# S5 loop: TensorE takes the two parts of each input matrix apart and adds them in PSUM, instead of VectorE adding them first

## What is computed

```python
a_r, a_i = mag * cos(lam_im * dt), mag * sin(lam_im * dt)
bb = coef * b                                  # complex, per group of 16 channels
bur, bui = einsum('gnh,btgh->btgn', bb, u)     # 64 groups, 64 complex states
x = associative_scan(a, bu) in chunks          # state over time
y = einsum('ghn,btgn->btgh', c_re, xr) - einsum('ghn,btgn->btgh', c_im, xi)
y = gelu(y + d * u)
```

## Time and profile before

| | us |
|---|---|
| median of 2 runs | 1878.67 |
| the two runs | 1875.09, 1882.25 |
| the profiled execution | 1876.33 |
| its span, first to last instruction | 1874.2 |
| TensorE busy | 1827.6 |
| VectorE busy | 850.5 |
| ScalarE busy | 778.3 |
| GpSimd busy | 883.0 |

### The profile page before, as it was taken

How to read it: one execution, slowest core, us unless ns; L and a number is a source line. 1 busy time by engine, 2 the same in 40 slices (tenths; PEclk the granted TensorE clock), 3 DMA queues, 4 the chain that set the end, 5 groups by cost and what they waited for, 6 DMA issues and landing times.

```text
span 1874.2 us, 24848 instructions
## 1 busy us (share of the span) xinstructions
PE 1827.6 (98%) x8784; PEld 1480.2 (79%) x8784; DVE 850.5 (45%) x1251; ACT 778.3 (42%) x1262; POOL 883.0 (47%) x1167
## 2 busy tenths in 40 slices
PE   5999999999999999999999999999999999999998
PEld 3688888888888777888888888788888878777876
DVE  8974232121126798432121126761355551477652
ACT  8854343232334567443232334423332342344663
POOL 1015455555545431555555545675454445573123
PEclk8899999999999999999999999999999999899999
DMA  5354243332333221334332323353322323241111
GB/s 193 101 178 149 90 144 103 91 101 90 101 92 99 88 74 39 91 101 146 90 101 90 101 92 93 92 168 90 90 79 79 90 70 106 65 124 57 35 57 56
DMA packets 56036, 182.50 MB, mean 97 GB/s; under 512 B 7200, under 2 KB 7584, under 8 KB 55312
## 3 DMA queue, kind: packets, MB, share of 16 engines
q1 hardware_dynamic: 52416, 174.44, 30.7%
q10 hardware_dynamic: 3536, 6.92, 1.1%
HBM read 165.93 MB, written 6.29 MB: 92 GB/s over the span
## 4 chain that ended last, share of the span: by engine, by line
PE 36%; POOL 29%; issue 28%; DVE 3%; ACT 2%; DMA 1%; POOLq 0%; SPq 0%; ACTq 0%; DVEq 0%
POOL wlo L550 29%; PE ps L1083 8%; PE ps L1085 7%; PE ps L1084 7%; PE ps L1477 2%; PE ps L1476 2%; PE ps L1475 2%; PE ps L1594 1%; PE ps L1584 1%; PE ps L1585 1%; PE ps L1132 1%; PE ps L1331 1%; PE ps L1148 1%; PE ps L1299 1%; PE ps L1522 0%
## 5 line engine op out<-in xcount | busy, mean ns | idle before, releaser
L550 POOL TENSOR_TENSOR wlo<-raw,whi 128x256 fp32r<-128x256 f32 x1136 | 860.0, 793 | 940.5 <-ACT whi L605 830.8
L605 ACT ACTIVATE whi<-raw 128x1024 fp32r<-128x1024 f32 x284 | 297.9, 1052 | 392.9 <-PE ps L1085 347.7
L1083 PE MATMUL ps<-Ch,whi 128*128 128x512 f32 x768 | 305.3, 398 | 0.6 <-POOL wlo L550 0.6
L1085 PE MATMUL ps<-Ch,wlo 128*128 128x512 f32 x768 | 299.3, 390 | 0.0
L1084 PE MATMUL ps<-Cl,whi 128*128 128x512 f32 x768 | 299.1, 389 | 0.0
L1083 PE MATMUL ps<-Ah,whi 128*128 128x512 f32 x632 | 251.8, 398 | 1.8 <-DVE Al L1824 1.6
L1083 PE MATMUL ps<-Bh,whi 128*128 128x512 f32 x640 | 250.4, 391 | 0.0
L1085 PE MATMUL ps<-Bh,wlo 128*128 128x512 f32 x640 | 249.0, 389 | 0.0
L1084 PE MATMUL ps<-Bl,whi 128*128 128x512 f32 x640 | 249.0, 389 | 0.0
L1085 PE MATMUL ps<-Ah,wlo 128*128 128x512 f32 x632 | 246.3, 390 | 0.0
L1084 PE MATMUL ps<-Al,whi 128*128 128x512 f32 x632 | 246.0, 389 | 0.0
(11 more groups left out here) (381 smaller groups left out, 2309.1 us busy)
## 6 DMA issues: line engine op xcount, KB each, us to landing
raw<-in_w SPq DMA_DIRECT2D x284, 512.0 KB, 3.6
ple<-ple_park SPq DMA_DIRECT2D x16, 256.0 KB, 3.9
ple_park<-E ACTq DMA_DIRECT2D x11, 256.0 KB, 2.2
u<-in_xch SPq DMA_DIRECT2D x1, 2048.0 KB, 8.5
swap<-vsb SPq DMA_DIRECT2D x16, 128.0 KB, 2.3
swap<-zz SPq DMA_DIRECT2D x16, 128.0 KB, 2.7
h<-in_xfm SPq DMA_DIRECT2D x2, 1024.0 KB, 6.7
out<-v SPq DMA_DIRECT2D x8, 256.0 KB, 2.0
```

Of the source, the lines that this page charges most:

```text
L550: last = nc.gpsimd.tensor_tensor(wlo[:, r, cc], raw[:, r, cc], whi[:, r, cc].bitcast(F32), ALU.subtract)
L605: nc.scalar.activation(whi[:, slot, :], raw[:, slot, :], ACT.Copy).then_inc(hi_ready, 1)
L1083: nc.tensor.matmul(out, whi[:, slot, w], xh, start=first, stop=False)
L1085: return nc.tensor.matmul(out, wlo[:, slot, w], xh, start=False, stop=last)
```

## The change

`inputs(sl)` calls `matrices` with the operation `None`: the sum (L345) and the wait before it are gone. The two products stay unsummed, the first in `E[:, sl%2]`, the second in `G2` for even slices and in `bt` for odd ones. In `transpose_inputs` each transpose becomes two plain fp32 matmuls with the identity moving, one for each part, accumulated in PSUM. In `kernel_products` each matmul becomes two, one for each part, accumulated in PSUM. Before, the second half of slice 6's kernel products ran in slice 7; now all 8 groups of each slice run in their own slice. `outputs(0)`, which writes its second part to `G2`, now waits until the kernel products of slice 6 are done (`e_used` at 7).

```diff
+        def input_parts(sl):
+
+            return E[:, sl % 2, :, :], (G2[:, :, :], bt[:, :].rearrange("p (g n) -> p g n", g=SG))[sl % 2]
...
                     for g in range(4):
-                        last = nc.tensor.transpose(ps[:, 2 + half, g * P:(g + 1) * P], E[:, sl % 2, 4 * half + g, :], C("ident"))
+                        for k, part in enumerate(input_parts(sl)):
+                            last = nc.tensor.matmul(ps[:, 2 + half, g * P:(g + 1) * P], part[:, 4 * half + g, :], C("ident"), start=(k == 0), stop=(k == 1))
                     last.then_inc(et_ps, 1)
 
             def kernel_products(sl, first, end):
                 for g in range(first, end):
                     gg = sl * SG + g
-                    last = nc.tensor.matmul(ps[:, gg // 32, gg % 32 * GH:(gg % 32 + 1) * GH], E[:, sl % 2, g, :], bC[:, 0, gg * GH:(gg + 1) * GH],
-                                            start=True, stop=True)
+                    for k, part in enumerate(input_parts(sl)):
+                        last = nc.tensor.matmul(ps[:, gg // 32, gg % 32 * GH:(gg % 32 + 1) * GH], part[:, g, :], bC[:, 0, gg * GH:(gg + 1) * GH],
+                                                start=(k == 0), stop=(k == 1))
...
                 pe.wait_ge(c_ready, 1)
-                if sl == NSL - 1:
-                    kernel_products(sl - 1, SG // 2, SG)
-                kernel_products(sl, 0, SG // 2 if sl == NSL - 2 else SG)
+                kernel_products(sl, 0, SG)
...
-                matrices(V, ch, E[:, sl % 2, :, :].rearrange("p g n -> p (g n)"), bt[:, :], pEr, sEi, 0, b1, b2, gs, ALU.add).then_inc(e_ready, 1)
+                one, two = (part.rearrange("p g n -> p (g n)") for part in input_parts(sl))
+                matrices(V, ch, one, two, pEr, sEi, 0, b1, b2, gs, None).then_inc(e_ready, 1)
...
                 if sl == 0:
                     dve.wait_ge(ple_ps, KT)
+                    dve.wait_ge(e_used, NSL - 1)
```

## The result

The changed kernel takes 1911.38 us (median of 1910.42 and 1912.34) against 1878.67 us before: 1.0192 times, 95% interval 1.0176 to 1.0208. It is slower by 1.9%. The forecast was 1898 us with a range of 1889 to 1911; the direction was right, and the time lies 13 us above the forecast and just over the range. The interval takes in 1.02, so it is left open whether the loss passes two per cent.

What follows compares the result with a forecast made beforehand. TensorE was taken to set the pace everywhere in the changed loop. The profiled 1876.3 us plus 15 at full clock plus 7 for clock falls gave 1898 us, with a range of 1889 to 1911.

Steps and rivals of the forecast that it cites:

- What bounds the loop: In the changed loop TensorE sets the pace everywhere: 14.0 us for a three-tile slice, against under 11 for VectorE.
- The gain: VectorE's eight removed sums in the loop make 9.8 us, gained only where TensorE waits for VectorE.
- The price of a pass: TensorE's loop passes at full clock: 0.111 us for transposing products, 0.106 for kernel products; 3.55 and 3.4 us a slice.
- The rival by the factor of four: Transposes in the loop: a plain fp32 matmul costs 0.44 us, not 0.22; total 1926 us, chance within 4%.
- The sum at full clock: TensorE's loop passes add to 94.3 us from 29.3 us; kernel products end at 123.6 us, 16.5 later than before.
- Start, order, tail: Around the loop: first slice gains nothing, reordering and new wait cost nothing, way to the product at 120.31 shrinks 1.6 us.
- The clock: Two falls behind the loop's long 16-column stretches, each some 7 us at half clock, 3.5 us lost: +7 us.
- +17: Upper bound of the loop's clock loss in us: five falls, or three of the long ones.
- The prediction's own sign of being wrong: In the loop: L1110 passes 0.2 us apart at full clock, half clock in most slices, or TensorE still waiting for VectorE.
- The case of a fall behind nearly every stretch: Five or more clock falls behind the loop's kernel products: 1908 us, with seven 1916; chance 25%.
- nearer +15: If transpose mode doesn't count as busy, the change helps the clock in the loop: nearer +15 than +22 us.

Runs made afterwards that it cites:

- e10: Changed kernel without the second part: VectorE adds nothing, TensorE takes only the first part in transposes and kernel products; 1874.50 us, 1.0001 of before.
- e7: Changed kernel, with one group of kernel products behind every second group of transposes and the last four groups behind them all; 1900.87 us.
- e1: Changed kernel, but the kernel products take the first part alone, while transposes stay two plain matmuls a group; 1887.03 us.
- e8: Kernel before the change, with each transpose made a plain fp32 matmul with the identity (two passes in place of one); 1875.10 us.
- e9: Kernel before the change, with each transpose issued twice into the same place; 1877.68 us.
- e2: Changed kernel, but each transpose is one transpose of the first part, while kernel products keep both parts; 1891.68 us.

## Why the prediction was off

- **What bounds the loop.** Right, and stronger than said: TensorE is busy for 119.3 of 120.3 us. The wait on `e_used` shows in five slices, 27 us of VectorE's time, hidden.
- **The gain.** The prediction named 9.8 us, but only where TensorE waits for VectorE, and put nothing of it into its sum. The condition was right: e10 puts the gain at nothing, with 1.5 us as the bound.
- **The price of a pass.** Transposing products 0.223 us a pair of passes, 3.57 us a slice (forecast 3.55). The L1594 rows were the right neighbours. Kernel products 3.50 us a slice, forecast 3.4: their passes stand 0.111 apart, not 0.106, for only the first pair of a stretch comes sooner (66.84 to 66.99 us). The slice at 86.05 us, with two tiles, has a fall; at full clock the terms give 1.82 + 3.5 + 3.57 + 3.5 = 12.4, and it took 14.06 with 3.4 us at half clock, of which 1.7 are lost.
- **The rival by the factor of four.** The Trainium skill, "TensorE: Matmul & The Clock Gate", Terms, has transpose mode four times faster for FP32. The trace doesn't agree: here a transpose took 0.11 us and the plain matmul with the same operands 0.22: a factor of two.
- **The sum at full clock.** Forecast 25.0 to 123.6, thus 98.6 us; measured 99.8. The missing 1.2 us are the kernel products' 0.1 us a slice, and some more.
- **Start, order, tail.** Input products at 29.53 us (forecast 29.3). End of the loop to the product on `T`: 145.4 to 157.0, 11.6 us (forecast 11.7). From there 19.0 us to the weight products, as before. The wait of `outputs(0)` was hidden, as argued. The 11.7 us are in part luck: they were added up over ScalarE, VectorE and the DMAs into `T`, but TensorE has no idle time between 146.94 us and the product at 156.99, so its own list set that start, with 3.4 us at half clock in it. Before, it still waited 0.23 us for the DMA there.
- **The clock.** This is the step that failed: "I expect some falls behind these: two, each some 7 us at half clock, 3.5 us lost, so +7". The place was right, the count was not. There were seven in the loop, five of 6.8 us and two of 3.4, 41 us at half clock, 20.5 us lost. The bound written beside it, "+17" for five falls, was too low too, and the range ended there. The error is 13.5 us in this term and 1.2 in the sum. Together they are the 14.8 us by which the loop ended late (145.4 against 123.6 + 7). Summed anew from what was measured, 15 + 1.2 + 20.5 = 36.7 us, against 36.0 between the profiled executions. The time lies so near the end of the range only because two of the seven falls were short; with seven long ones it would be 3.4 us more (an estimate, 2 x 1.7). The prediction's own sign of being wrong, half level in most slices, came true in seven of eight.
- **Why it was mis-sized.** The case of a fall behind nearly every stretch stood as a rival with 25% (seven falls at 1916 us, as all were taken as long ones), against it "full clock from 77 to 107 us". But in that part a slice had 1.7 us of kernel products and up to 5.2 us of PLE. The new slices have twice the kernel products. The one old row like them was the fall at 39.2 us with 0.7 us of idle, and it spoke for the rival. The split order, which brings back stretches of 1.7 us, showed that the order of the passes is what counted: with it the kernel takes 1895.3 us, inside the range. Its two falls, e7's three and e1's four show that short stretches are not enough to say when the clock holds.

The same page, "Part 4: PE-mode transpose", says transpose mode doesn't count as busy for the full clock; the prediction noted that the sum would by that be nearer +15. It was not: with all transposes plain the clock fell seven times. Between the profiles of e8 and e9, where only the mode differs, the loops' mean clocks are equal; the single runs leave a small effect open.

## What to carry to other kernels

When work moves to TensorE, count the passes, and then ask in what order the narrow and the dense ones will stand: here eight stretches of 32 passes of 16 columns, 28 us in all, came with 20.5 us of lost clock, and splitting them around a block of dense passes gave 16 us back for a change of order alone. Before paying an engine's time to relieve another, run the kernel with the relieved work simply left out: here that showed that eight sums of 1.2 us were worth 1.5 us at most. Look at the mean clock of every execution, too, before reading a cause from one trace: e2's trace was its worst run by 7 us. A likely fall of the clock in a loop should be priced once for each slice at the upper end, not for two of eight.

## What the runs showed of the hardware

- TensorE's granted clock can fall to half without idle time before it. In the changed kernel it fell seven times in a loop in which TensorE was busy for 99% of the time: four times in the last passes of a stretch of 32 sixteen-column passes (3.5 us), three times within 2.0 us behind one. The same passes in the split order had two falls, 6.8 us at half clock in place of 41.
- A pass of an fp32 matmul with 128 weights stood 0.11 us from the next at full clock, whether 16 or 128 columns moved; one of 512 columns took 0.433 us. Sixteen columns are as dear as 128.
- Added passes can be nearly free: 64 more in the loop of the kernel before (7 us of passes) changed its time by 0.0001 of it (plain matmuls) and 0.0011 (doubled transposes), while the mean clock of the loop rose from 0.85 to 0.92.
- The same kernel can lose more to the clock in one execution than in another: e8's ten runs go from 1872.5 us at a mean clock of 0.995 to 1878.5 us at 0.990.
- Open: why the finer interleaving had twice the half-clock time of the split order, and what part the input products behind the kernel products have in the falls.
